# The MLP of a decoder step: 26 of 32 pairs of output tiles as seven block products each

## What is computed

```
mix = jnp.concatenate([ret_y, nsa_y], -1) @ w_o
h = x + rmsnorm(mix, ln_post_mix)
f = jnp.square(jax.nn.relu(rmsnorm(h, ln_pre_ffn) @ w_up)) @ w_down
return h + rmsnorm(f, ln_post_ffn)
```

## Time and profile before

| | us |
|---|---|
| runs of the kernel (median; lowest, highest) | 1816.93; 1815.42, 1817.02 |
| span of the profiled execution (first to last instruction) | 1813.8 |
| TensorE busy in it (94% of the span) | 1701.5 |
| DVE, ACT, POOL busy | 837.9, 617.7, 147.4 |
| the tail, from its first matmul | 939.5 to 1813.8 |

### The profile page before, as it was taken

One profiled execution on the slowest core, in us unless ns is written; L12 is line 12 of the kernel. 1 busy time (PEld: TensorE's weight loads), 2 busy tenths in 40 slices (PEclk: granted clock), 3 DMA queues, 4 the chain that ended last, 5 costly groups with the idle time before them and its releaser, 6 DMA issues. The chain is left out here.

```text
span 1813.8 us, 29538 instructions
## 1 busy us (share of the span) xinstructions
PE 1701.5 (94%) x11632; PEld 1512.8 (83%) x11632; DVE 837.9 (46%) x1611; ACT 617.7 (34%) x1189; POOL 147.4 (8%) x257
## 2 busy tenths in 40 slices
PE   5999999995999679999989999999999999999997
PEld 4989988995874556565559889999999999999997
DVE  5556342131126367777866674322332233223466
ACT  5222322210010156666655554202320232023343
POOL 1000000003534300000000110000000000000011
PEclk9999999998999789999999999999999999999999
DMA  8111011144967500000036542111111111111455
GB/s 294 47 48 48 24 48 42 47 105 119 246 174 200 145 15 1 1 1 1 1 88 180 168 123 83 59 47 48 47 47 47 48 47 47 47 47 47 118 173 164
DMA packets 215949, 148.99 MB, mean 82 GB/s; under 512 B 13565, under 2 KB 205394, under 8 KB 215426
## 3 DMA queue, kind: packets, MB, share of 16 engines
q1 hardware_dynamic: 180050, 99.38, 19.4%
q0 software_dynamic: 12720, 37.21, 6.6%
q10 hardware_dynamic: 23040, 10.50, 2.3%
HBM read 134.76 MB, written 16.47 MB: 83 GB/s over the span
## 5 line engine op out<-in xcount | busy, mean ns | idle before, releaser
L2145 PE MATMUL psum<-act_hi,whi 128*128 128x344 f32 x952 | 306.7, 322 | 5.0 <-issue 5.0
L2145 PE MATMUL psum<-act_hi,wlo 128*128 128x344 f32 x952 | 304.0, 319 | 0.0
L2145 PE MATMUL psum<-act_lo,whi 128*128 128x344 f32 x952 | 304.0, 319 | 0.0
L2262 DVE TENSOR_TENSOR wlo<-wraw,whi 128x1024 fp32r<-128x1024 f32 x111 | 136.1, 1226 | 255.7 <-ACT whi L2160 255.5
L2145 PE MATMUL psum<-hidden_hi,whi 128*128 128x344 f32 x768 | 246.4, 321 | 0.0
L2145 PE MATMUL psum<-hidden_hi,wlo 128*128 128x344 f32 x768 | 245.3, 319 | 0.0
L2145 PE MATMUL psum<-hidden_lo,whi 128*128 128x344 f32 x768 | 245.2, 319 | 0.0
L2160 ACT ACTIVATE whi<-wraw 128x1024 fp32r<-128x1024 f32 x111 | 117.5, 1059 | 339.8 <-PE psum L2145 326.4
L235 PE MATMUL psum<-act_hi,whi 128*128 128x344 f32 x648 | 214.0, 330 | 4.0 <-DVE act_lo L408 4.0
L235 PE MATMUL psum<-act_hi,wlo 128*128 128x344 f32 x648 | 207.6, 320 | 0.0
L235 PE MATMUL psum<-act_lo,whi 128*128 128x344 f32 x648 | 207.5, 320 | 0.0
(11 more groups left out here) (390 smaller groups left out, 2473.8 us busy)
## 6 DMA issues: line engine op xcount, KB each, us to landing
wraw<-in_w_down SPq DMA_DIRECT2D x48, 512.0 KB, 3.6
wraw<-in_w_up SPq DMA_DIRECT2D x40, 512.0 KB, 4.0
wraw<-in_w_in SPq DMA_DIRECT2D x27, 512.0 KB, 3.8
wraw<-in_w_o SPq DMA_DIRECT2D x23, 512.0 KB, 3.8
h_features<-mixed_then_h POOLq DMA_DIRECT2D x24, 172.0 KB, 2.4
h_again<-h_features POOLq DMA_DIRECT2D x24, 172.0 KB, 2.8
x_rows<-in_x_prompt SPq DMA_DIRECT2D x4, 1024.0 KB, 9.3
dec_pages<-in_cache_sel_k SPq DMA_DIRECT2D x64, 64.0 KB, 3.3
```

Source lines behind the costliest of these rows:

```text
L2145: last = pe.matmul(ps[:, u % 3, 0:TN], wt[:, kt, :], xt[:, kt, cols], start=(kt == 0 and i == 0), stop=(kt == KT - 1 and i == 2))
L2262: dve.tensor_tensor(m.wlo[p % 2][:], wraw[raw_slot[p]][:], m.whi[p % 2][:].bitcast(F32), ALU.subtract).then_inc(lo_ready, 1)
```

## The change

14 pairs of hidden tiles of `w_up` and 12 pairs of output tiles of `w_down` (3 of the 4 quarters, now called slabs) are computed by Strassen's scheme in Winograd's form. A pair is a product of a 2 x 2 block matrix of weights (blocks of 128 outputs by 512 inner) and a 2 x 2 block matrix of activations (blocks of 512 inner by `HT` = 516 tokens). It is made of seven products of one left and one right block or sum of blocks, instead of eight. Of slab 3, hidden tiles 0 to 3 stay as 12 units behind the 24 of `w_o` (`head_tiles`); hidden tiles 4 to 7 are the pairs 0 and 1; slabs 0, 1, 2 are the pairs 2 to 13. Then come the `down` pairs 14 to 25, slabs 0, 1, 2; then `down` of slab 3 as 24 units, as before.

- **PE.** A product is 24 matmuls: 2 halves of 258 columns x 4 inner tiles x 3 products of high and low parts. 26 x 7 = 182 products replace 156 units. Their sums over products are formed partly in PSUM (products 3 to 6 are added to the banks of 1, 0, 1, 2) and partly by DVE.
- **Left operands.** One weight load of 1 MB per pair. POOL forms four sums of blocks (`left_sum`); ACT rounds and DVE subtracts for each of the seven products (`left_hi`, `left_lo`: 128 x 512), four products ahead, in five slots.
- **Right operands of `up`.** ACT scales h in place by the norm's gains (`scale_x`, 24 instructions), DVE forms three differences and POOL one (each 128 x 2064), and all four are split; the low parts are made three quarters on DVE, one quarter on POOL.
- **Results of an `up` pair.** One copy (ACT) and six PSUM reads (DVE), three ReLUs, four squares, and for slabs 0 to 2 four differences (DVE): the seven right operands of the `down` pairs. SP stores them to DRAM (`hidden_forms`); slab 3 goes there as plain blocks (`hidden_last`).
- **Right operands of `down`.** For each slab SP loads the seven forms (each 128 x 2064 float32, 1.06 MB), ACT rounds them, DVE and POOL make the low parts, in place of the previous slab's, form by form behind the last products that use them. For slab 3 four blocks are loaded.
- **Results of a `down` pair.** DVE adds into `mlp_out`; from the second slab on POOL makes three more additions of 128 x 516 per pair (`add_to_y`).

`hidden_hi` and `hidden_lo` no longer exist; `mlp_out` lies where h was.

```diff
+HT = TOK // 2
+SLABS = 3
+PAIRS = 4
+FORMS = 7
+UP_PAIRS = SLABS * PAIRS + 2
...
+BANKS = (0, 2, 4, 2, 0, 2, 4)
+LEFT_SUM = {1: 1, 2: 0, 3: 2, 6: 3}
...
+def form_loads():
+
+
+    first = FORMS * (UP_PAIRS - 1)
+    out = []
+    for i, free, load, split in ((0, 1, 2, 4), (1, 2, 3, 5), (2, 3, 4, 6), (4, 0, 5, 7), (3, 5, 6, 8), (5, 0, 6, 9), (6, 6, 7, 10)):
+        out.append((0, i, first + free, first + load, first + split))
+    for s in range(1, SLABS + 1):
+        last = FORMS * (UP_PAIRS + PAIRS * s - 1)
+        for i in range(FORMS if s < SLABS else PAIRS):
+            out.append((s, i, last + i, last + i + 1, last + i + 3))
+    return out
+
+
...
+            def load_form(slab, i, free):
...
+                sp.wait_ge(product_done, free + 1)
+                src = f_forms[slab, i] if slab < SLABS else f_last[:, 2 * i:2 * i + 2, :].rearrange("p k (e n) -> p (k e) n", e=2)
+                sp.dma_start(right_f[i][:], src).then_inc(f_loaded[i], 16)
...
+            def left_sum(g, i):
+
+                at = 4 * g
+                to = sums_up if g < 16 else sums_down
+                a11, a12, a21, a22 = (block_of(g, out, k) for out in range(2) for k in range(2))
+                if i == 0:
+                    pool.wait_ge(pair_loaded[g % 2], 16 * (g // 2 + 1))
+                    if g == 16:
+                        pool.wait_ge(product_done, FORMS * UP_PAIRS)
+                if g:
+                    pool.wait_ge(form_lo, FORMS * (g - 1) + (3, 3, 4, 7)[i])
+                if i == 0:
+                    pool.tensor_tensor(to[0][:], a21, a22, ALU.add).then_inc(left_sums, 1)
+                elif i == 1:
+                    pool.wait_ge(left_sums, at + 1)
+                    pool.tensor_tensor(to[1][:], to[0][:], a11, ALU.subtract).then_inc(left_sums, 1)
+                elif i == 2:
+                    pool.tensor_tensor(to[2][:], a11, a21, ALU.subtract).then_inc(left_sums, 1)
+                else:
+                    pool.wait_ge(left_sums, at + 2)
+                    pool.tensor_tensor(to[3][:], a12, to[1][:], ALU.subtract).then_inc(left_sums, 1)
+
...
+            def form_lo_part(n):
+                slab, i, *_ = loads[n]
+                pool.wait_ge(f_form_hi, n + 1)
+                pool.tensor_tensor(right_lo[i][:, 3:4, :], right_f[i][:, 3:4, :], right_hi[i][:, 3:4, :].bitcast(F32),
+                                   ALU.subtract).then_inc(f_form_lo_pool, 1)
...
+            def bank_wait(g, pos):
+                if pos == 0:
+                    if g:
+                        pe.wait_ge(psum_read, 6 * g - 2)
+                    else:
+                        pe.wait_ge(evacuated, NU - NO)
+                        pe.wait_ge(h_ready, 3 * KT)
+                        pe.wait_ge(rstd_ready, 3)
+                elif pos == 1 and g:
+                    pe.wait_ge(psum_read, 6 * g - 1)
+                elif pos == 2 and g:
+                    pe.wait_ge(psum_read, 6 * g)
+                elif pos == 3:
+                    pe.wait_ge(psum_read, 6 * g + 1)
+                elif pos == 4:
+                    pe.wait_ge(first_copied, g + 1)
+                elif pos == 5:
+                    pe.wait_ge(psum_read, 6 * g + 2)
+                elif pos == 6:
+                    pe.wait_ge(psum_read, 6 * g + 3)
...
+            for at in range(PRODUCTS):
+                g, pos = divmod(at, FORMS)
+                bank_wait(g, pos)
+                if g == 0 and pos in (1, 2, 3, 5):
+                    i = (1, 2, 3, 5).index(pos)
+                    pe.wait_ge(x_form_lo, i + 1)
+                    pe.wait_ge(x_form_lo_pool, i + 1)
+                if g >= UP_PAIRS and down_place(g)[1] == 0:
+                    n = next(n for n, form in enumerate(loads) if form[0:2] == (down_place(g)[0], pos))
+                    pe.wait_ge(f_form_lo, n + 1)
+                    pe.wait_ge(f_form_lo_pool, n + 1)
+                pe.wait_ge(form_lo, at + 1)
+                w_hi, w_lo = left_hi[at % SLOTS], left_lo[at % SLOTS]
+                x_hi, x_lo = right_operand(g, pos)
+                for e in range(2):
+                    cols = slice(e * (HT // 2), (e + 1) * (HT // 2))
+                    for kt in range(4):
+                        for i, (wt, xt) in enumerate(((w_hi, x_hi), (w_hi, x_lo), (w_lo, x_hi))):
+                            last = pe.matmul(ps[:, BANKS[pos] + e, 0:HT // 2], wt[:, kt, :], xt[:, kt, cols],
+                                             start=(pos < 3 and kt == 0 and i == 0), stop=(kt == 3 and i == 2), skip_group_check=True)
+                last.then_inc(product_done, 1)
+
...
+            def x_differences():
+
+                b11, b12, b21, b22 = (hT[:, 4 * k:4 * k + 4, half(e)] for k in range(2) for e in range(2))
+                dve.wait_ge(scaled, 3 * KT)
+                dve.wait_ge(h_totals, 3)
+                dve.wait_ge(h_summed, 6)
+                dve.tensor_tensor(right_f[1][:], b12, b11, ALU.subtract).then_inc(x_diffs, 1)
+                dve.wait_ge(x_diffs, 1)
+                dve.tensor_tensor(right_f[0][:], b22, right_f[1][:], ALU.subtract).then_inc(x_diffs, 1)
+                dve.wait_ge(x_diffs, 2)
+                dve.tensor_tensor(right_f[3][:], b21, right_f[0][:], ALU.subtract).then_inc(x_diffs, 1)
...
+            for at in range(PRODUCTS):
+                g, pos = divmod(at, FORMS)
+                if pos == 0 and g:
+                    take_c12(g - 1)
+                    if g <= UP_PAIRS:
+                        relu(g - 1, 2)
+                elif pos == 2:
+                    take_u2(g)
+                elif pos == 4:
+                    take_u3(g)
+                elif pos == 5:
+                    take_c11(g)
+                    if g < UP_PAIRS:
+                        relu(g, 0)
+                elif pos == 6:
+                    take_c21(g)
+                    if g < UP_PAIRS:
+                        relu(g, 1)
+                if at + LEAD < PRODUCTS:
+                    left_lo_of(at + LEAD)
+                if pos == 2:
+                    differences(g - 1, (0,))
+                elif pos == 3:
+                    differences(g - 1, (1, 2, 3))
+                if at in (1, 3):
+                    x_lo_of(2 + at // 2)
+                for n, (_, _, _, _, split_at) in enumerate(loads):
+                    if split_at == at:
+                        form_lo_of(n)
+                if at == PRODUCTS - 3:
+                    last_reduce(0)
```

More of the change, by code:

```diff
@@ L1897, in stage_tail @@
-        raw_use = [raw_slot[:p + 1].count(raw_slot[p]) for p in range(len(tiles))]
-        kind = [tiles[p][0] for p, c in units]
-        number = [sum((kind[v] == "o") == (kind[u] == "o") for v in range(u + 1)) for u in range(NU)]
-        ups = [u for u in range(NU) if kind[u] == "up"]
-        up_number = {u: n + 1 for n, u in enumerate(ups)}
-        f_need = {(tiles[units[u][0]][1], units[u][1]): up_number[u] for u in ups}
-        last_down = [u for u in range(NU) if kind[u] == "down" and tiles[units[u][0]][1] == QUARTERS - 1]
@@ L1905, in stage_tail @@
-        y_number = {u: n for n, u in enumerate(last_down)}
-        y_start = last_down[0]
+        tiles = head_tiles()
+        NU = len(tiles)
+        NO = 3 * KT
+        FIRST = 4
+        raw_slot = [FIRST if p == 0 else p % 4 if p < NO else p % 2 for p in range(NU)]
+        raw_use = [raw_slot[:p + 1].count(raw_slot[p]) for p in range(NU)]
+        loads = form_loads()
+        NL = 3 * KT
         SUB = TN // 4
         T8 = KT * TOK * 4
+        H4 = HT * 4
+        B4 = H4 + 16
         C4 = TN * 4
+        lo, ring = m.tables, m.ring
@@ L2117, in behind_last @@
                     turn_y(c, 0)
-            for u, (p, c) in enumerate(units):
-                k, j = place_of(u)
-                if k is not None:
-                    behind_chunk(k, j)
+            for u in range(NL):
+                c, n = divmod(u, KT)
                 k, j = y_place_of(u)
@@ L2167, in evacuate @@
             def evacuate(u):
-                p, c = units[u]
-                what, q, n, _ = tiles[p]
+                what, n, c = tiles[u]
                 if what == "o":
@@ new lines, in take_c21 @@
+            def take_c21(g):
+                dve.wait_ge(product_done, FORMS * g + 6)
+                if g < UP_PAIRS:
+                    at = part = wide(f21[g % 2])
+                else:
+                    slab, n = down_place(g)
+                    at = y_part(2 * n + 1, 0)
+                    part = wide(first_d) if slab == 0 else at
+                    if slab:
+                        dve.wait_ge(y_pool, 3 * (g - UP_PAIRS - PAIRS) + 1)
+                dve.tensor_tensor(at, part, banks(1), ALU.add).then_inc(psum_read, 1)
@@ new lines, in take_c12 @@
+            def take_c12(g):
+                dve.wait_ge(product_done, FORMS * g + 7)
+                if g < UP_PAIRS:
+                    at = part = wide(f12[g % 2])
+                else:
+                    slab, n = down_place(g)
```

(5 more changed lines are left out.)

672 lines of the change are left out of this document (533 added, 139 removed).

## The result

The changed kernel takes **1825.89 us**, the median of 18 runs (1820.43 to 1830.27); the kernel before took 1816.97 in the 18 runs beside it. The ratio is **1.0038**, with a 95% interval from 1.0029 to 1.0048: slower by 0.4%. I had predicted 1777.0 us, and 1760 to 1815 as the range.

What follows compares the result with a forecast made beforehand. PE's instruction stream was taken as the bound from 1105 us to the end of the units. 1813.8 - 61.4 + 10.5 + 5 + 5 + 1 = 1773.9 us of span, plus 3.1 gives 1777.0 us; range 1760 to 1815.

Steps and rivals of the forecast that it cites:

- products for units: Tail: 156 units (589.2 us) give way to 182 products of 2.90 us (527.8 us): -61.4 us, ends -58 and -76.
- head, up to product 3: Before and in the first products: PE waits for unit 35 and first operands, plus a lowered clock: +10.5 us (5 to 18).
- `up` to `down`: Change from `up` to `down` pairs: DVE exceeds PE's time and transfers are tight: +5 us (1 to 9).
- first, second change of slab: Between slabs of `down`: DVE recovers no backlog and the second form lands some 2 us late: +2.5 us each (0 to 5).
- last slab and units: Change to the last slab with four forms: +1 us; last 24 units and what follows as before: 0.
- Steady pairs at nothing: Pairs away from head and changes: PE's 20.3 us cover the work of DVE, ACT and POOL, so no cost.
- The rival with its condition and its rows: Head and changes: POOL and DVE instructions with both inputs in SBUF cannot run at once; 1800 us, chance 0.24.
- The clock: Behind the head's gap: PE's clock is lowered for about 3 us, as at the tail's start; 1.5 us added.
- Theory D: Changes of operands: forms arrive late from DRAM whatever POOL does; 1822 to 1829 us expected with POOL nearly idle.

Runs made afterwards that it cites:

- pool_writes: Changed kernel with each POOL tensor instruction of the tail made a memset of the same output tile, reading nothing: 1781.35 us, 0.9807 of the kernel before.
- pool_copies: Changed kernel with each POOL tensor instruction of the tail made a copy of one SBUF input to the same tile: 1797.17 us, 0.9889 of the kernel before.
- all_dve: Changed kernel with every POOL tensor instruction of the tail (sums, additions, third difference, low parts) moved to DVE: 1809.82 us, 0.9952 of the kernel before.
- lo_quarter: all_dve with its head reordered twice, and DVE's low parts for slabs 0 to 2 covering one tile of four: 1781.18 us, 0.9793 of the kernel before.

## Why the prediction was wrong

The two spans differ by +7.7 us. In the kernel before, the chain's piece of 166 units begins with unit 35, so the first replaced unit starts at 1105.34 + 3.78 = 1109.1, and the last 24 units start at 1732.35 - 9 x 3.777 = 1698.4. In the changed kernel these marks are 1129.45 and 1700.53. For the changes of operands I take the starts of ACT's copy of each pair's first product. A pair without a wait takes 20.15 us from copy to copy, as here; across the first change there are two longer steps:

```profile
1385.42 0.60 ACT L2571 ACTIVATE pair_out<-psum 128x516 f32<-128x516 f32 x1 [1.65 <-PE psum L2416]
1405.57 0.60 ACT L2571 ACTIVATE pair_out<-psum 128x516 f32<-128x516 f32 x1 [1.65 <-PE psum L2416]
1430.80 0.58 ACT L2571 ACTIVATE down_first<-psum 128x516 f32<-128x516 f32 x1
1462.88 0.60 ACT L2571 ACTIVATE down_first<-psum 128x516 f32<-128x516 f32 x1 [2.17 <-PE psum L2416]
```

25.23 and 32.08 us, so 5.1 + 11.9 = 17.0 too long. The same for the other places and kernels, in us:

| term | predicted | change | pool_writes | pool_copies | all_dve | lo_quarter |
|---|---|---|---|---|---|---|
| products for units | -61.4 | -65.4 | | | | |
| head, up to product 3 | +10.5 | +28.8 | | | | |
| unit 32 to product 3, whole | | 48.6 | 38.4 | 40.3 | 44.7 | 34.9 |
| `up` to `down` | +5 | +17.0 | 6.9 | 9.0 | 13.0 | 4.7 |
| first, second change of slab | +2.5, +2.5 | +10.1, +8.9 | 0.8, 1.0 | 4.9, 5.2 | 7.3, 7.2 | 0, 0 |
| last slab and units | +1 | +8.3 | | | | |

- **The products:** right, and a little better than said: 26 pairs of 20.15 us are 523.9 us in place of 589.3. A matmul of 258 columns takes 119.7 ns, between my two ends (117.5 and 121.6).
- **Steady pairs at nothing:** right. No pair away from the head and the changes is longer than 20.17 us, even though 42 relu rows of DVE take 1211 ns instead of 693. Cover hides exclusion where there is slack.
- **The step that failed:** "I stay with the sum, since a blocked instruction may often fall into a time in which the engine would have waited for its semaphore anyway." With it the blocked time was put at nothing. At the changes no engine had such a time: from 1523 to 1540 DVE was busy for 17.00 and POOL for 16.86 of 17 us, their blocked time included, and took turns. The rival with its condition and its rows was written down, "DVE rows of 512 elements that take over 0.9 us where POOL is busy, or POOL rows well over 1.1", and both came (1.17 and 1.75; 1.7 to 2.8), yet it had a chance of 0.24. Its prices for the changes of slab, 7 and 9 us, are near the 10.1 and 8.9 measured; for `up` to `down` it said 10 and 17.0 came. Its whole, 1800 us, was also short: with POOL's measured 1.27 us per row in place of 1.1 its sum gives some 1808 us, and what is still missing to 1826 lies in the head, at `up` to `down` and in the last slab.
- **Without the exclusion the sum holds at these places:** pool_writes loses 6.9, 0.8 and 1.0 us, where I had said 5, 2.5 and 2.5, and its whole time, 1781.35 us, is 4 us from the 1777.0. That nearness is partly luck: its head is about 8 us dearer than my 10.5 and the products 4 us cheaper than my sum. Its POOL rows are also shorter, 0.53 us, but the copies of 0.61 us alone show that length is not what matters.
- **The head was mis-sized even without exclusion.** 28.8 us are 20.3 until product 0 and 8.5 in products 0 to 2. From unit 32's start to product 3's, pool_writes takes 38.4 us (1098.10 to 1136.54), so 10.2 of the 48.6 are POOL's. I had counted the three differences in a row as given; making them in DVE's idle time, with the emptying of units put ahead of them, saves another 9 us on top of all_dve. About 4 us lie ahead of unit 32: it starts at 1097.98, and three units' time ahead of the start of unit 35 before would be 1105.34 - 3 x 3.777 = 1094.0. Of these, 0.6 us lie ahead of the tail (its first matmul starts at 940.03 and, before, at 939.47). The rest comes where ACT's scalings stand ahead of its rounding of weights, so that DVE waits 1.77 us for each weight tile (`tail_hi`) and, before, 0.40 (`whi`); I had counted none. That the scalings cause it was not tried. The third norm's factor now waits 1.89 us for `h_diagonal`, uncounted too.
- **The clock** was right in kind, short in number: I counted one loss of 1.5 us. After each wait of over 5 us the granted clock is lowered again: the stretches that hold the waits show 0.84, 0.90, 0.85 and 0.81, and 1700 to 1710, with a wait of 2.71 us, has 0.77, where the kernel before has 1.00. That stretch is most of the last term: from the start of the last 24 units to the end it is 121.0 us against 115.4 before, so the wait of 2.71 us on POOL's `right_lo` costs 5.6 with the clock.
- **Theory D:** I priced the changes by transfers landing late. They do land late (7.7 us in the median, where rows 10 have 7.0 for a megabyte), but lo_quarter shows that with DVE relieved this costs 3 to 5 us once, and nothing from slab to slab. With DVE full, the idle time that it leaves in DVE adds up to some 2 us at a change.

The terms as measured add up: -65.4 + 28.8 + 17.0 + 10.1 + 8.9 + 8.3 = +7.7 us. The last one is what the marks leave over, so the sum closes by construction.

## What to carry to other kernels

Before moving work from VectorE to GpSimd, ask whether both will read SBUF at once in a stretch without slack: if so, add their times, and GpSimd's are the longer ones. A stretch where the sum of the coupled engines exceeds TensorE's time shows as waits on DVE in a kernel that looks 58% busy. And price the changes between steady stretches before the stretches themselves: here 65 us of gain were spent in five short places.
